# Delta rule in a decoder trunk: the inversion of the 16x16 blocks in seven items of the hand-written order in place of three, and its transposed copy on ScalarE

## What is computed

```python
A = jnp.where(strict, jnp.einsum('nbhid,nbhjd->nbhij', kb, k) * decay, 0.0)
rhs = jnp.concatenate([v * beta[..., None], kb * jnp.exp(gc)[..., None]], -1)
sol = lax.linalg.triangular_solve(jnp.eye(C, dtype=jnp.float32) + A, rhs,
                                  left_side=True, lower=True, unit_diagonal=True)
...
def squared_relu_mlp(h, w1, w2):
    return jnp.square(jax.nn.relu(h @ w1)) @ w2
```

## Time and profile before

| | |
|---|---|
| median of 3 runs | 2660.91 us (2659.46 to 2661.53) |
| profiled execution | 2657.77 us, span 2656.0 us |
| TensorE busy | 2582.1 us (97%) |
| TensorE weight loads | 2301.5 us (87%) |
| VectorE busy | 1385.4 us (52%), 2209 instructions |
| ScalarE busy | 1127.5 us (42%) |
| GpSimd busy | 249.9 us (9%) |
| mean granted clock of TensorE | 0.991 |

### The profile page before, as it was taken

How to read it: one execution, slowest core, us unless ns; L and a number is a source line. 1 busy time by engine, 2 the same in 40 slices (tenths; PEclk the granted TensorE clock), 3 DMA queues, 4 the chain that set the end, 5 groups by cost and what they waited for, 6 DMA issues and landing times.

```text
span 2656.0 us, 39212 instructions
## 1 busy us (share of the span) xinstructions
PE 2582.1 (97%) x16262; PEld 2301.5 (87%) x16262; DVE 1385.4 (52%) x2209; ACT 1127.5 (42%) x1915; POOL 249.9 (9%) x402
## 2 busy tenths in 40 slices
PE   7998989899999999999999999999999999999998
PEld 5778988788787798899999989998877888999998
DVE  4746774656564465534454465535544456444344
ACT  5564446455444244433333345433332344333324
POOL 5121111100101001100000001110000000000000
PEclk8999999999999999999999999999999999999999
DMA  6454335533323345543333245554434334233322
GB/s 188 158 156 114 109 105 142 154 93 94 104 88 100 113 141 161 177 127 100 116 88 105 88 124 156 171 143 130 119 119 144 103 115 127 84 110 110 96 88 82
DMA packets 368721, 321.47 MB, mean 121 GB/s; under 512 B 11929, under 2 KB 339667, under 8 KB 368544
## 3 DMA queue, kind: packets, MB, share of 16 engines
q1 hardware_dynamic: 336224, 207.91, 26.9%
q0 software_dynamic: 32320, 111.05, 13.4%
HBM read 261.33 MB, written 57.58 MB: 120 GB/s over the span
## 4 chain that ended last, share of the span: by engine, by line
PE 83%; DVE 7%; ACT 5%; issue 2%; DMA 1%; POOL 1%; DVEq 0%; ACTq 0%; POOLq 0%
PE dense L591 74%; PE mixer L591 8%; DVE wlo L1627 2%; ACT arena L1116 1%; ACT whi L1116 1%; DVE arena L1849 1%; DMA proj<-ffh 0%; DVE ffh L1666 0%; ACT relu L1116 0%; ACT ffh L1116 0%; DVE hf L1765 0%; DVE arena L1851 0%; ACT L1116 0%; DMA arena<-xrow 0%; DVE hlo L1761 0%
## 5 line engine op out<-in xcount | busy, mean ns | idle before, releaser
L591 PE MATMUL dense<-hhi,whi 128*128 128x272 f32 (+1 forms) x3072 | 850.8, 331 | 29.4 <-DVE wlo L1627 19.0
L591 PE MATMUL dense<-hlo,whi 128*128 128x272 f32 (+1 forms) x3072 | 826.5, 323 | 0.0
L591 PE MATMUL dense<-hhi,wlo 128*128 128x272 f32 (+1 forms) x3072 | 826.4, 323 | 0.0
L1627 DVE TENSOR_TENSOR wlo<-wst,whi 128x1024 fp32r<-128x1024 f32 x384 | 469.4, 1222 | 242.7 <-ACT whi L1116 241.7
L591 PEld LDWEIGHTS dense<-hhi,whi 128*128 128x128 f32 x3072 | 516.6, 189 | 89.4 <-DVE wlo L1627 24.8
L1116 ACT ACTIVATE whi<-wst 128x1024 fp32r<-128x1024 f32 x384 | 403.7, 1051 | 419.9 <-PE dense L591 416.0
L591 PEld LDWEIGHTS dense<-hhi,wlo 128*128 128x128 f32 x3072 | 515.4, 189 | 42.5
L591 PEld LDWEIGHTS dense<-hlo,whi 128*128 128x128 f32 x3072 | 517.8, 189 | 37.4 <-issue 0.7
L591 PE MATMUL dense<-h1hi,whi 128*128 128x272 f32 (+1 forms) x1536 | 422.6, 329 | 12.5 <-DVE wlo L1627 8.1
L591 PE MATMUL dense<-h1hi,wlo 128*128 128x272 f32 (+1 forms) x1536 | 414.3, 324 | 0.0
L591 PE MATMUL dense<-h1lo,whi 128*128 128x272 f32 (+1 forms) x1536 | 412.2, 323 | 0.0
(11 more groups left out here) (348 smaller groups left out, 1808.5 us busy)
## 6 DMA issues: line engine op xcount, KB each, us to landing
wst<-in_w_ff_dram SPq DMA_DIRECT2D x256, 512.0 KB, 4.0
wst<-in_w_in_even_dram SPq DMA_DIRECT2D x48, 512.0 KB, 4.0
wst<-in_w_in_odd_dram SPq DMA_DIRECT2D x48, 512.0 KB, 3.9
proj<-ffh POOLq DMA_DIRECT2D x48, 272.0 KB, 2.4
proj<-ffh POOLq DMA_DIRECT2D x48, 256.0 KB, 2.3
arena<-proj POOLq DMA_DIRECT2D x16, 512.0 KB, 4.7
wst<-in_w_out_even_dram SPq DMA_DIRECT2D x16, 512.0 KB, 3.6
arena<-proj POOLq DMA_DIRECT2D x8, 1024.0 KB, 8.1
```

The source lines that it names most:

```text
L591: return pe.matmul(out, lhsT, rhs, start=start, stop=stop)
L1627: TT(wlo[:, u % 2, :], wst[:, u % 2, :], whi[:, u % 2, :].bitcast(F32), ALU.subtract)\
```

## The change

The three items `b1`, `b2`, `b3` of each tile become `b1`, `b1b`, `b2`, a rest, `b2b`, `b3`, `b3b`, and one of the five rests that followed goes (with `b4`, which stays as it is, these are the seven items of the title). `b1` keeps only the four small steps on the 4x4 blocks. The two left products of 4x4 blocks are `b1b`, the two right ones `b2` (so the scratch `U` holds both), the left product of 8x8 blocks is `b2b`, the right one `b3`. The transposed copy becomes `b3b`, done by ScalarE, which waits for VectorE's last reduction; GpSimd waits for ScalarE's copy and stands at `b3b`. `g_inv` counts four signals for a tile in place of three.

```diff
-            out += [("rest",)] * 1 + [("g", t, s, 0) for s in ("b1", "b2", "b3")] + [("rest",)] * 5
+            out += [("rest",)] * 1
+            for s in ("b1", "b1b", "b2", "b2b", "b3", "b3b"):
+                out += [("g", t, s, 0)] + [("rest",)] * (s == "b2")
+            out += [("rest",)] * 4
...
+                elif step == "b3b":
+                    w("inv", t * (4 + 2 * NL) + 1)
+                    c = m["C"][:, 0:WB * WB].rearrange("p (i j) -> p i j", j=WB)
+                    s(A_(m["CT"].rearrange("p (j i) -> p i j", i=WB), c, ACT.Copy), "inv")
...
-                link(dve.tensor_reduce(out, tmp, mybir.AxisListType.X, ALU.add))
...
+                ins = dve.tensor_reduce(out, tmp, mybir.AxisListType.X, ALU.add)
+                if linked:
+                    link(ins)
+                return ins
...
-                    for s_ in range(WB // 8):
-                        merge_left(m, 8 * s_, 4)
-                        merge_right(m, 8 * s_, 4)
-                elif step == "b2" and LB == 4:
-                    merge_left(m, 0, 8)
+                elif step == "b1b":
+                    for a in range(2):
+                        u = m["U"][:, 16 * a:16 * a + 16].rearrange("p (i c) -> p i c", i=4)
+                        product(m, u, block_of(m, 8 * a + 4, 8 * a, 4), block_of(m, 8 * a, 8 * a, 4), 4)
+                elif step == "b2":
+                    for a in range(2):
+                        u = m["U"][:, 16 * a:16 * a + 16].rearrange("p (i c) -> p i c", i=4)
+                        product(m, block_of(m, 8 * a + 4, 8 * a, 4), block_of(m, 8 * a + 4, 8 * a + 4, 4), u, 4)
+                elif step == "b2b":
+                    u = m["U"].rearrange("p (i c) -> p i c", i=8)
+                    product(m, u, block_of(m, 8, 0, 8), block_of(m, 0, 0, 8), 8)
                 elif step == "b3":
-                    if LB == 4:
-                        merge_right(m, 0, 8)
-                    c = m["C"][:, 0:WB * WB].rearrange("p (i j) -> p i j", j=WB)
-                    s(dve.tensor_copy(m["CT"].rearrange("p (j i) -> p i j", i=WB), c), "inv")
+                    u = m["U"].rearrange("p (i c) -> p i c", i=8)
+                    s(product(m, block_of(m, 8, 0, 8), block_of(m, 8, 8, 8), u, 8, False), "inv")
...
-                    pool.wait_ge(S("g_inv"), t * (3 + 2 * NL) + 1)
+                    pool.wait_ge(S("g_inv"), t * (4 + 2 * NL) + 2)
...
-                if t < TILES and name in ("kk", "b3"):
+                if t < TILES and name in ("kk", "b3b"):
```

12 lines of the change are left out of this document (3 added, 9 removed).

## The result

The changed kernel took 2667.84 us (median of 9 runs, 2664.43 to 2671.95) against 2660.53 us for the kernel before in the same rounds (2659.46 to 2661.53): ratio 1.0032, 95% interval 1.0023 to 1.0040 (the quotient of the two medians is 1.0027). It is slower, by 7 us, where 2.3 less had been forecast, and its runs lie 7.5 us apart where those of before lie 2.

What follows compares the result with a forecast made beforehand. TensorE, busy nearly throughout, was taken as the bound, held up by late weights and the inversion's chain. Terms -3.8 - 0.2 + 1.4 + 0 + 0.3 = -2.3 us gave 2658.6 us against a median of 2660.91; range 2653.0 to 2664.5.

Steps and rivals of the forecast that it cites:

- Tile 0: `b1` partly fits into VectorE's 3.46 us gap ahead of a `lo`, so the inversion ends earlier: -0.2 us.
- Tile 1: Tile 1's chain: A +1.1, blocks to finished inverse +0.3, so `la` starts later: +1.4 us, bounds -0.9 and +2.
- Tile 2: `b3b` ends some 0.6 us later than the copy did, but `b4` has slack: 0.
- Tile 3: The 5.11 us `lo` wait is split between weights and `b4`; `lb` starts 0.3 us later; bounds -1 and +2.5.
- Tiles 4 to 6: TensorE's waits for `lo` (3.5 us) and tile 5's for `b4` (0.7) go: -3.8 us, bounds 0 and 4.2.
- The copy: ScalarE's transposing copy of 256 elements: 0.39 us plus 0.1 hand-over, against VectorE's 0.37; chain some 0.1 longer per tile.
- no wait for `lo` near 518 and 687: Sign in tiles 4 to 6: TensorE's waits at units 61 and 85, 1.57 and 1.55 us, are gone.
- some 3 us for it in tile 3: Sign in tile 3: TensorE's wait for `lo` is about 3 us in place of 5.11.
- the wait in tile 1: Sign in tile 1: TensorE's wait for `b4` is still 7 us or more.
- that for `b4` in tile 3: Sign in tile 3: a new TensorE wait for `b4` of about 2 us before `la`.
- Rival 2: Tiles 0 to 3 lose over 4 us behind ScalarE's queue, tiles 4 to 6 win nothing: 6 slower, 2667; chance 0.16.
- rival 3: Round trip by bytes: a DMA costs the same each time, tile 1 wins 1.4 us back: 2657.2; chance 0.10.

Runs made afterwards that it cites:

- experiment 3: Against the kernel before: seven items only in tiles 4 to 7, three in tiles 0 to 3, VectorE's copy everywhere; 2659.00 us, ratio 1.0001.
- experiment 11: Against the kernel before: only tile 3's inversion in the changed order's places and form, with ScalarE's copy; 2661.69 us, ratio 1.0011.
- Experiment 14: Against the kernel before: only `b3` of tiles 4 and 6 one piece later, behind `lo(61)` and `lo(85)`; 2654.99 us, ratio 0.9985.
- experiment 18: Against the changed kernel: ScalarE's copy does not transpose, so dependent results are wrong; 2659.93 us, one run.
- experiment 2: Against the kernel before: its three items kept, only the copy behind `b3`'s product moved to ScalarE; 2665.66 us, ratio 1.0027.

## Why the prediction was wrong, step by step

The forecast (-2.3 in all) priced engines and let each trip through DRAM take what it took before. The steps that failed are those of tiles 0 and 3, forecast at -0.2 and +0.3 and measured at +4.7 and +4.6, and in both the same assumption: that the round trip of the inverse and the clock stay as they were. Tile 0 had no bound above 0 at all. By the traces, changed against before, the chain of each tile up to `b4`, and then to level 6:

- **Tile 0, -0.2 forecast, +4.7 measured.** The inversion ended 0.03 us later, so VectorE's part was right. The copy took 0.28 us more, store and load 2.2 and 0.65 more: +3.2 until `b4`. The clock's fall added 1.6. The sentence that `b1` "partly fits into that gap" looked at VectorE alone and forgot that SyncE issues weights when `lo` ends: `lo(21)` 0.9 us late, those weights 2 us late.
- **Tile 1, +1.4 forecast, +2.8 measured.** Until `b4` it is +1.5: A +1.0, and GpSimd's queue +0.75 and +0.67, since a send now stands ahead of either store (at 228.38 and 246.14 in the timeline above), the copy +0.28, and 0.2 inside the inversion, against 1.3 of shorter trips. That the sum fits the +1.4 is luck, for its terms do not: GpSimd's queue was not walked through. The remaining 1.3 is the clock, and it appears in experiments 3 and 11 too, where tile 1 is as before (1.1 and 1.4 us between `b4` and level 6), so it is scatter rather than the change.
- **Tile 2, 0 and +0.5.**
- **Tile 3, +0.3 forecast, +4.6 measured.** The split inside the chain is +2.1 and the copy +0.28, against 2.4 forecast: right. `b1` started another 0.7 later (the store of A took 0.65 longer, its load 1.4; a step of the convolution ended with it, and which of the two held `b1` is not shown), and the second trip took 1.2 more: neither was in the forecast. With them `b4` came 4.3 later, where the forecast had 2.4 and let the slack before `lb` take up all but 0.3; that supposed full clock, and TensorE stood 4.60 us for `b4`, not about 2, and then worked at 0.59. Alone (experiment 11) this tile costs 4.1 in the trace and 3.1 in the time. The second fall stood in the prediction only as the bound of +2.5, though TensorE was to stand for 2 us right behind a stretch at 0.53.
- **Tiles 4 to 6, -3.8 forecast, -2.4 measured.** All three waits for `lo` went, as forecast, and tile 5's for `b4`; 2.5 us came back in a new wait for `lo` (0.57 at 844), the wait for `b4` of tile 7, the sample's `sum` and a longer one for ScalarE. Experiment 14 won 3.7 with nothing else moved.
- **The copy**, 0.39 forecast, 0.66 measured. The 0.39 is the plain copy of experiment 18 (0.41). The Trainium skill (VectorE: DVE Perf Modes, "The TRN2 errata — SBUF-src ops pay a fixed extra latency per instruction") gives 0.40 as an estimate from its 224 cycles and the elements; the plain copy agrees, the transposing one does not.

Of the signs named, no wait for `lo` near 518 and 687, some 3 us for it in tile 3 and A of tile 1 about 1 us later came true; the wait in tile 1 (6.54, not 7 or more), that for `b4` in tile 3 (4.60, not about 2) and the copy (0.66, not 0.35 to 0.45) did not. One slip in the range: half of tile 3's bound of 2.5 is 1.25, not 1.6; the measured time lies above either end.

Rival 2, the chain pays more, is the nearest, with 0.16 of the chances. The fall of the clock while TensorE works was in it; its reason, a copy behind ScalarE's queue, was not the case in the changed kernel (the copy starts 0.03 us behind the product). Its size of 6 was near the 7 by luck: tiles 0 to 3 lost twice what it had for them, and tiles 4 to 6 won 2.4 where it had nothing. The premise of rival 3, a DMA costs the same each time, fell clearly: 64 KB stores took 2.2 to 5.8 us in one place. The Trainium skill (DMA: Bandwidth & Descriptors, "Anatomy of one DMA — SWDGE (gpsimd) path") has about 2.0 us and the bytes, which makes 2.15 for 64 KB, an estimate from that page; the undisturbed stores of 2.2 us agree, the undisturbed loads of 3.0 and all the others do not.

What stays open: why stores with like neighbours differ by 1 to 2 us, how much of tile 0's loss is the order of GpSimd's transfers and how much their time, what beside the wait decides whether the clock falls, and why experiment 2's median is 7 us up where its trace has 5 (its profiled execution is the fastest of its eight).

## What to carry to other kernels

A step that is moved ahead of a buffer's release moves the transfer that this release starts. Walk every queue past it, the DMA queues too, and ask which transfer of the critical chain now meets which bulk transfer. In experiment 2, 0.28 us of copy in each tile grew to 5.4 us in the trace: by the weights behind the copy in ScalarE's queue, by longer loads, and by the clock.

Where TensorE will stand for a chain, price the chain's lengthening with the fall of the clock behind it, not only with the wait. And to take away one wait, move the one item that makes it: two items moved by one piece won 3.7 us, a whole list spread anew lost 7.

## What was not expected of the hardware

- ScalarE's copy of 32x256 fp32: 0.66 us with a stride of 16 on its write or its read, 0.41 without; VectorE does the strided one in 0.37.
- A store of 64 KB from GpSimd's queue took 2.2 us in nine traces and 3.0 to 5.8 in the eleven where the weight transfers around it lay otherwise; the load behind it took 3.0 to 5.0.
- The clock dips to half for about 3 us, costing 1.6, at 1760 or near 2090 us in some executions and not in others of kernels that are alike there; TensorE had been busy for 15.5 of the 16 us before (before, 2060 to 2076) or all of them (experiment 3, 1735 to 1751).
